# A two-block network on one Trainium2 core: the transposed inverse of the gated delta rule turned in 32x32 blocks on VectorE

## The reference

```python
def gated_delta_rule(q, k, v, beta, log_decay):
...
    kb = k * beta[..., None]
    a_low = jnp.where(strict, jnp.einsum('bhnid,bhnjd->bhnij', kb, k) * decay_mat, 0.0)
    eye = jnp.eye(c, dtype=jnp.float32)
    t_mat = lax.linalg.triangular_solve(eye + a_low, jnp.broadcast_to(eye, a_low.shape),
                                        left_side=True, lower=True, unit_diagonal=True)
    w_c = jnp.matmul(t_mat, kb * jnp.exp(gc)[..., None])
    u_c = jnp.matmul(t_mat, v * beta[..., None])
```

## Time and profile before

| what | value |
| --- | --- |
| runs | 3604.08, 3609.72 and 3613.27 us, median 3609.72 |
| span of the profiled execution, first to last instruction | 3607.4 us |
| own time of the profiled execution | not given apart from its span |
| TensorE busy, share of the span | 3446.0 us, 96% |
| VectorE busy | 1998.2 us, 55% |
| ScalarE busy | 715.4 us, 20% |
| mean granted TensorE clock | 0.978 of full speed |
| the inversion | 203.5 to 274.7 us of the span |

### The profile page before, as it was taken

How to read it: one execution, slowest core, us unless ns; L and a number is a source line. 1 busy time by engine, 2 the same in 40 slices (tenths; PEclk the granted TensorE clock), 3 DMA queues, 4 the chain that set the end, 5 groups by cost and what they waited for, 6 DMA issues and landing times.

```text
span 3607.4 us, 43951 instructions
## 1 busy us (share of the span) xinstructions
PE 3446.0 (96%) x16699; PEld 2722.7 (75%) x16699; DVE 1998.2 (55%) x4671; ACT 715.4 (20%) x1763; POOL 88.1 (2%) x105
## 2 busy tenths in 40 slices
PE   8987999999999999999998988999999999999988
PEld 3484788888754568888887766888887888887766
DVE  4472367554404784675544558643354656558566
ACT  2231021100013551211001135022212011121143
POOL 0000000000000000000000021000000000000110
PEclk9998999999999999999999999999999999999999
DMA  3200312222210003122222220212211222102311
GB/s 130 82 13 27 125 47 82 94 82 94 105 47 36 16 33 118 58 82 82 94 82 82 71 83 24 82 71 77 74 65 45 102 74 89 41 24 84 112 42 48
DMA packets 39975, 254.09 MB, mean 70 GB/s; under 512 B 5796, under 2 KB 5924, under 8 KB 11616
## 3 DMA queue, kind: packets, MB, share of 16 engines
q1 hardware_dynamic: 31616, 224.41, 17.6%
q0 software_dynamic: 3664, 15.07, 1.2%
q10 hardware_dynamic: 4496, 11.89, 1.2%
HBM read 242.68 MB, written 2.18 MB: 68 GB/s over the span
## 4 chain that ended last, share of the span: by engine, by line
PE 88%; DVE 8%; issue 2%; ACT 1%; DMA 1%; ACTq 0%; POOL 0%; POOLq 0%; DVEq 0%
PE PL L1212 26%; PE PX L1212 20%; PE PL L923 14%; PE PL L1560 4%; PE PL L1407 3%; PE PL L907 2%; PE PX L1669 2%; DVE SCR L2972 2%; PE PL L1325 1%; DVE SCR L2987 1%; PE PL L1585 1%; PE PX L1345 1%; PE PL L1712 1%; PE PL L1374 1%; PE PX L933 1%
## 5 line engine op out<-in xcount | busy, mean ns | idle before, releaser
L923 PE MATMUL PL<-xn,ring 128*128 128x264 f32 (+1 forms) x1600 | 501.6, 471 | 11.2 <-DVE xn L2366 10.7
L923 PEld LDWEIGHTS PL<-xn,ring 128*128 128x128 f32 x1600 | 304.4, 192 | 193.7 <-issue 161.8
L2409 DVE TENSOR_TENSOR Z<-PL,SCR 128x512 f32<-128x512 f32 (+3 forms) x104 | 63.9, 614 | 447.0 <-PE PL L923 349.2
L1212 PE MATMUL PL<-Z,ring 128*128 128x256 f32 (+1 forms) x1248 | 297.4, 389 | 10.4 <-DVE Z L3362 8.6
L1212 PEld LDWEIGHTS PL<-Z,ring 128*128 128x128 f32 x1248 | 241.3, 194 | 49.8 <-DVE Z L3362 9.7
L1212 PE MATMUL PL<-AUX,ring 128*128 128x256 f32 (+1 forms) x1056 | 243.9, 379 | 0.0
L1212 PEld LDWEIGHTS PL<-AUX,ring 128*128 128x128 f32 x1056 | 200.6, 190 | 27.6 <-DVE AUX L2740 0.2
L1212 PE MATMUL PL<-xn,ring 128*128 128x264 f32 (+1 forms) x864 | 204.2, 389 | 12.7 <-DVE xn L2366 11.6
L1212 PEld LDWEIGHTS PL<-xn,ring 128*128 128x128 f32 x864 | 165.8, 192 | 42.9 <-issue 12.1
L1840 ACT ACTIVATE SCR<-PL 128x256 f32<-128x256 f32 (+1 forms) x72 | 27.6, 383 | 737.2 <-PE PL L1212 737.2
L1212 PE MATMUL PX<-Z,AUX 128*128 128x264 f32 (+1 forms) x704 | 163.8, 384 | 2.7 <-DVE Z L3170 2.7
(11 more groups left out here) (514 smaller groups left out, 6043.3 us busy)
## 6 DMA issues: line engine op xcount, KB each, us to landing
ring<-w_tiles SPq DMA_DIRECT2D x212, 1024.0 KB, 4.8
Z<-Z ACTq DMA_DIRECT2D x16, 264.0 KB, 5.0
SCR<-head_rows POOLq DMA_DIRECT2D x16, 264.0 KB, 3.7
AUX<-norm_scratch POOLq DMA_DIRECT2D x8, 528.0 KB, 6.6
cst<-consts ACTq DMA_DIRECT2D x1, 2188.5 KB, 15.4
resid<-x ACTq DMA_DIRECT2D x4, 512.0 KB, 9.3
Z<-norm_scratch POOLq DMA_DIRECT2D x4, 512.0 KB, 8.0
AUX<-mem POOLq DMA_DIRECT2D x2, 1024.0 KB, 5.1
```

The source lines that it names most:

```text
L923: mm = pe.matmul(PL[:, 2 * h + c, 0:e - a], ring[t % 2][:, k, P * h:P * h + P], src_block(name, k)[:, a:e], start=k == 0, stop=k == KB - 1)
L1212: mm = pe.matmul(ps, lhs(k), rhs(k), start=kc == 0 and k == 0, stop=kc == per - 1 and k == 3)
L2409: ins = dve.tensor_tensor(d, ps, f, ALU.mult)
```

## The change

`Tm` and `Um` are transposes of each other. While both are block diagonal with blocks of up to 32, VectorE's transpose, which turns each 32x32 block of a tile by itself, makes the one from the other. `BY_BLOCK` is 20, the first step of the level of block length 32.

- In level 0, TensorE's transposes are gone. VectorE makes `Um` (`unit_less_first`) and turns it into `Tm` (`turned_blocks`).
- In the steps 4 to 19, TensorE makes no product for `Um`. VectorE subtracts from `Tm` (`subtracted`) and turns it into `Um` (`turned_blocks`), which now raises `dn_inv`.
- From step 20 on, both products and subtractions are as before.
- `dn_yps` is counted from step 4 on, and the waits for it are shifted by four.
- VectorE's order in the levels 1 to 6 is now: subtraction of n-1, `couple(n + 1)`, turn of n-1.
- TensorE waits for the last copy of the transposed keys (`kv_sb` at 8) ahead of all steps.

```diff
--- before.py
+++ after.py
@@ -524,6 +524,7 @@
 
 
         H4 = 4
+        BY_BLOCK = 4 * LEVELS.index(32)
         gcB, betaB, egB = (Z1[:, a:a + 4] for a in (0, 4, 8))
         qgB = X1[:, 0:4]
         pool_y = Z1[:, 20:24]
@@ -1090,30 +1091,24 @@
                         pe.wait_ge(dn_inv, n - 1)
                     if n < last:
                         for h in range(H4):
-                            pe.matmul(PL[:, 2 * (n % 2), P * h:P * h + P], Um[:, c, h, :], Yb[n % 2][:, h, :],
-                                      start=True, stop=True)
+                            mm = pe.matmul(PL[:, 2 * (n % 2), P * h:P * h + P], Um[:, c, h, :], Yb[n % 2][:, h, :],
+                                           start=True, stop=True)
                     for h in range(H4):
-                        mm = pe.matmul(PL[:, 2 * (n % 2) + 1, P * h:P * h + P], Yb[n % 2][:, h, :], Um[:, c, h, :],
-                                       start=True, stop=True)
+                        if n >= BY_BLOCK:
+                            mm = pe.matmul(PL[:, 2 * (n % 2) + 1, P * h:P * h + P], Yb[n % 2][:, h, :], Um[:, c, h, :],
+                                           start=True, stop=True)
                     mm.then_inc(dn_tu, 1)
 
-                for n in range(n_all):
+                pe.wait_ge(kv_sb, 8)
+                for n in range(4, n_all):
                     c = n % 4
                     pe.wait_ge(dn_bt, n + 1)
-                    if n == 1:
-                        pe.wait_ge(kv_sb, 8)
-                    if n >= 4:
-                        pe.wait_ge(dn_inv, n - 3)
-                    if 2 <= n < 6:
-                        pe.wait_ge(dn_inv, n - 1)
-                    elif n >= 6:
+                    pe.wait_ge(dn_inv, n - 3)
+                    if n >= 6:
                         pe.wait_ge(dn_y, n - 5)
                     for h in range(H4):
-                        if n < 4:
-                            mm = pe.transpose(PX[:, n % 2, P * h:P * h + P], BTb[n % 2][:, h, :], ident)
-                        else:
-                            mm = pe.matmul(PX[:, n % 2, P * h:P * h + P], BTb[n % 2][:, h, :], Tm[:, c, h, :],
-                                           start=True, stop=True)
+                        mm = pe.matmul(PX[:, n % 2, P * h:P * h + P], BTb[n % 2][:, h, :], Tm[:, c, h, :],
+                                       start=True, stop=True)
                     mm.then_inc(dn_yps, 1)
                     if n >= 5:
                         apply(n - 1)
@@ -1975,7 +1970,7 @@
                 act.wait_ge(psum_free, evacuated("a_in"))
                 mark(act.activation(Z1[:, 16:20, :], Z1[:, 16:20, :], ACT.Silu))
                 for n in range(4, len(LEVELS) * 4):
-                    act.wait_ge(dn_yps, n + 1)
+                    act.wait_ge(dn_yps, n - 3)
                     if n >= 6:
                         act.wait_ge(dn_tu, n - 5)
                     act.activation(Yb[n % 2], PX[:, n % 2, :].rearrange("p (h d) -> p h d", h=4), ACT.Copy).then_inc(dn_y, 1)
@@ -2855,35 +2850,55 @@
 
                 eye = ident.rearrange("p (a t) -> p a t", a=1).broadcast_to([P, 4, P])
 
-                def invert(n):
+                n_all = len(LEVELS) * 4
+
+                def subtracted(n):
+
                     c = n % 4
                     v = lambda x: x.rearrange("p (h d) -> p h d", h=4)
-                    if n < 4:
-                        dve.wait_ge(dn_yps, n + 1)
-                        dve.tensor_tensor(Tm[:, c], eye, v(PX[:, n % 2, :]), ALU.subtract).then_inc(dn_inv, 1)
-                        return
                     dve.wait_ge(dn_tu, n - 3)
-                    if n < len(LEVELS) * 4 - 4:
-                        dve.tensor_tensor(Tm[:, c], Tm[:, c], v(PL[:, 2 * (n % 2), :]), ALU.subtract)
-                    dve.tensor_tensor(Um[:, c], Um[:, c], v(PL[:, 2 * (n % 2) + 1, :]), ALU.subtract).then_inc(dn_inv, 1)
+                    if n < n_all - 4:
+                        counted(dve.tensor_tensor(Tm[:, c], Tm[:, c], v(PL[:, 2 * (n % 2), :]), ALU.subtract))
+                    if n >= BY_BLOCK:
+                        dve.tensor_tensor(Um[:, c], Um[:, c], v(PL[:, 2 * (n % 2) + 1, :]), ALU.subtract).then_inc(dn_inv, 1)
+
+                def turned_blocks(n):
+
+                    dve.wait_ge(dve_step, own[0])
+                    a, b = (Tm, Um) if n < 4 else (Um, Tm)
+                    dve.transpose(a[:, n % 4].rearrange("p h d -> p (h d)"), b[:, n % 4].rearrange("p h d -> p (h d)")
+                                  ).then_inc(dn_inv, 1)
 
                 def couple(n):
                     lv, c = n // 4, n % 4
                     m = K("levels", P * lv, P * lv + P).rearrange("p (a t) -> p a t", a=1).broadcast_to([P, 4, P])
-                    if n >= 2:
-                        dve.wait_ge(dn_yps, n - 1)
+                    if n >= 6:
+                        dve.wait_ge(dn_yps, n - 5)
                     dve.tensor_tensor(BTb[n % 2], ATm[:, c], m, ALU.mult).then_inc(dn_bt, 1)
-                    if lv == 0:
-                        dve.wait_ge(dn_bt, n + 1)
-                        dve.tensor_tensor(Um[:, c], eye, BTb[n % 2], ALU.subtract)
+
+                def unit_less_first(n):
+
+                    dve.wait_ge(dn_bt, n + 1)
+                    counted(dve.tensor_tensor(Um[:, n % 4], eye, BTb[n % 2], ALU.subtract))
 
                 couple(0)
-                for n in range(len(LEVELS) * 4):
-                    if n + 1 < len(LEVELS) * 4:
+                couple(1)
+                for n in (0, 2):
+                    unit_less_first(n)
+                    unit_less_first(n + 1)
+                    turned_blocks(n)
+                    couple(n + 2)
+                    turned_blocks(n + 1)
+                    if n == 0:
+                        couple(3)
+                for n in range(4, n_all):
+                    if n > 4:
+                        subtracted(n - 1)
+                    if n + 1 < n_all:
                         couple(n + 1)
-                    if n:
-                        invert(n - 1)
-                invert(len(LEVELS) * 4 - 1)
+                    if 4 < n <= BY_BLOCK:
+                        turned_blocks(n - 1)
+                subtracted(n_all - 1)
                 for c in range(4):
                     if c:
                         dve.wait_ge(st_x, c)
```

## The result

The changed kernel takes 3638.01 us (median of four runs, 3635.65 to 3642.37) against 3608.77 for the kernel before: the ratio is 1.008, with a 95% interval of 1.0068 to 1.0092. It is 29.2 us slower; 24.3 were forecast.

The account below looks back on a forecast made before the run. TensorE was taken to bound levels after the first, VectorE the first. Level 0 -0.35, block products 4 to 6 +0.76, from there to the state's first product +23.04, clock +0.8: +24.3 on 3609.72, 3634.0 us; range 3628 to 3660.

Parts of the forecast that it names:

- the ring: Levels 1 to 4: apply(n-1), subtraction(n-1), coupling(n+1), block product(n+1), apply(n) wait on each other in turn; 3.43 us against 2.68.
- Level 5: Steps n = 20 to 23 keep both apply groups and both subtractions, so a step takes 4.92 us.
- Level 0: Steps 0 to 3, set by VectorE: first coupling to block product 4 takes 7.55 us against 7.90, a gain of 0.35.
- the price of a turn: VectorE's 32x32-block turn of 128x512 taken as 0.60 us, the pace of nearby 512-column operations.
- The estimate of 1.24 us: Alternative time for VectorE's turn, from four 128x128 bf16 turns at 311 ns; would add 1.9 us to the sum.
- The cover in the ring: The turn, issued behind the coupling, costs nothing in levels 1 to 4 up to 2.23 us.
- The clock: TensorE's low clock around the first block products and apply group adds 0.8 us, the middle of nothing and 1.5.
- once up it should stay up: TensorE's clock keeps 1.00 despite pauses, as from 290 to 295 us with TensorE busy 2.42 of 5.00 us.
- The rival of the low clock: Clock stays at 0.50 through 15 turns after level 0, 24.6 us more, 3658.6 us; level 5 should end it; chance 0.16.
- one sign of being wrong: Among the signs listed against the forecast: the granted clock at 0.50 beyond 220 us.
- Behind the inversion: The state's products and the norm wait for the inversion's end, so all of it is later by the whole 24.3 us.
- The faster rival: Coupling n+1, issued ahead of apply n-1's end, is not held up: 14.4 us less with level 0, 3595.3 us; chance 0.04.

Follow-up runs that it names:

- The order alone: The kernel before, with VectorE issuing the subtraction of n-1 ahead of the coupling of n+1 from step 5 on, no turn: 3678.63 us, ratio 1.0189.
- VectorE's transpose with the old order: The changed kernel, with the coupling of n+1 again ahead of the subtraction of n-1: 3600.71 us, ratio 0.9976 to the kernel before.
- the pauses filled: The changed kernel, with 6 unused matmuls (4 in the last level) behind each apply group of levels 5 and 6: 3636.51 us, ratio 1.0074.

## Why the prediction was right

The sign, the place and the mechanism of the loss came out as forecast: the ring. Its size was 4.9 us short by the medians (29.2 against 24.3), and 8.9 by the two profiled spans (33.2); in the profiled run the clock, which was priced too low, makes most of that.

- **The ring.** Forecast 3.43 us for one turn of the ring, measured 3.43 to 3.44 in 15 of 15. The order alone makes a loss, and VectorE's transpose with the old order a gain: both were tried.
- **Level 5.** Forecast 4.92 us a step. This holds at the full clock (4.92 and 4.93 with the pauses filled); in the changed kernel three of four took 6.5.
- **Level 0 and the price of a turn.** Forecast 7.55 us with a turn of 0.60, measured 7.75. Of the 0.20 over, 0.15 lie in the last link, from coupling 4 (209.93) to block product 4 (210.81), 0.88 us against 0.73, and not in the turns. The value taken by the pace of the neighbouring operations was right. The estimate of 1.24 us, worked out from a bf16 price of the Trainium skill (VectorE: DVE Perf Modes, The three transpose paths), was twice too dear against the measured 0.60. The cover in the ring is real: a second turn cost nothing.
- **The clock.** This is the term that was mis-sized. The sum had 0.8 us for it, all at the start. Measured in the profiled run: 0.67 more between block products 4 and 6 (6.87 against 5.40 + 0.8), and 7.04 in levels 5 and 6 (three steps 1.63, 1.63 and 1.58 over, two 0.47 and 1.73). With 0.2 from level 0 that is 7.9 of the 8.0 us by which the inversion exceeds 95.5. For the medians this split is not shown, since only one run of the changed kernel was profiled. The step that failed reads "once up it should stay up": that held for the turns of 3.43 us from block product 6 to 21, with pauses of 1.57 us between the loads, and failed in level 5, with steps of 4.92 and pauses of 2.17. It rested on a row of another stage (290 to 295 us), which did not carry over. The rival of the low clock was priced for levels 1 to 4, where it did not come, and said that level 5 should end it, where it began; its price of 0.82 us a group was right (1.71 against 0.89). Taken by its words, one sign of being wrong was met, the clock at 0.50 beyond 220 us, though not in the levels that it was meant for. What the Trainium skill tells of another kernel (TensorE: Matmul & The Clock Gate, A second HAM failure mode), that short idles between groups of matmuls make the clock swing, is borne out by level 5 and by the order alone (steps of 6.55 us in place of 4.92), and not by levels 1 to 4 (3.43 us throughout).
- **Behind the inversion** nothing was taken up: 3334.0 us against 3332.7.
- **The faster rival** was decided at the point that was named. With the coupling issued ahead of the ring, the gain is there: 13.9 us of the inversion, against 14.4 forecast for that rival.

## What to carry to other kernels

Where two engines work in order, an operation moved past a wait also moves everything queued behind that wait: follow the new order once around both queues and add up the links before counting the work saved. Here two lines in the other order turned a gain of 8 us into a loss of 29, and issuing the coupling one step earlier made the gain 11.5. A stage that begins to pause also puts the clock of its matmuls at risk: give that a price in each loop for itself, and do not take it from another loop that kept the clock.

## What the runs showed of the hardware

The clock told two rather similar loops apart. With steps of 3.43 us and pauses of 1.57 it stayed at 1.00 from block product 6 to 21; with steps of 4.92 and pauses of 2.17 it fell and rose again from step to step, and such a step took 6.55 us. What decides between the two is not shown: level 6, behind that swing, has the links of levels 1 to 4 again and pauses of 1.68 us, and TensorE ran at 0.50 in it too (298 to 300 us). A fall in a ring costs what the groups on it lose, here two apply groups at 0.82 us each, since every later step waits for them. Matmuls without use, put into the pauses, gave back 21.5 us to the kernel with the order alone.

VectorE's turn of 32x32 blocks runs at the pace of a subtraction of the same shape: 0.60 us from start to start for 128x512 in float32, and 704 ns from start to end against 0.69 us.
